# Hybrid mixer trunk: four stretches of fill in the state stage, both outputs in one bank, and new orders at the LRU, the branches and the second norm

## What is computed

```
h = RMSNorm(x) * (1 + scale1) + shift1
p = h @ W_in                        # columns split among four mixers
o_b = mixer_b(p slice)              # RG-LRU, stick-breaking attention, gated DeltaNet, RWKV-7
x = x + gate1 * ( sum_b sigmoid(h W_gate_b + b_gate_b) * (o_b W_branch_b) ) @ W_out
h = RMSNorm(x) * (1 + scale2) + shift2
x = x + gate2 * ( (gelu(conv(h W_gate)) * (h W_up)) @ W_down )
final RMSNorm
```

```
u = u_first - w S            # new values, w from the keys
o = q S + (q k) u            # output
S = decay * S + k u          # new state
```

## Time and profile before

| | |
|---|---|
| runs | 1933.66, 1928.02, 1931.73 us; median 1931.73 |
| the profiled execution | 1933.4 us, span 1931.5 us |
| mean granted clock of PE | 0.994 |
| busy: PE, DVE, ACT, POOL | 97%, 48%, 24%, 48% of the span |
| chain that ended last | PE 84%, DVE 8%, ACT 2%, POOL 2%, transfers 2% |

### The profile page before, as it was taken

One profiled execution on the slowest core, in us unless ns is written; L12 is line 12 of the kernel. 1 busy time (PEld: TensorE's weight loads), 2 busy tenths in 40 slices (PEclk: granted clock), 3 DMA queues, 4 the chain that ended last, 5 costly groups with the idle time before them and its releaser, 6 DMA issues.

```text
span 1931.5 us, 33600 instructions
## 1 busy us (share of the span) xinstructions
PE 1880.7 (97%) x14138; PEld 1499.8 (78%) x14138; DVE 935.9 (48%) x1443; ACT 467.2 (24%) x731; POOL 921.6 (48%) x1100
## 2 busy tenths in 40 slices
PE   6999999999999999999999899999999999999997
PEld 3778777767787887887887787788888888888885
DVE  3965578754546546545545825532332322323326
ACT  3432344451212213213214314310110101101103
POOL 2876556523223223323324574464655555655655
PEclk9999999999999999999999999999999999999999
DMA  8625211232222122122135521111111111111112
GB/s 337 213 77 185 98 55 66 82 125 79 66 68 78 52 83 78 40 94 78 41 105 196 206 100 33 33 44 55 43 54 43 54 44 54 44 52 45 45 53 87
DMA packets 69976, 163.51 MB, mean 85 GB/s; under 512 B 6112, under 2 KB 30816, under 8 KB 69856
## 3 DMA queue, kind: packets, MB, share of 16 engines
q1 hardware_dynamic: 62368, 142.88, 22.2%
q10 hardware_dynamic: 7488, 18.88, 2.6%
HBM read 133.17 MB, written 28.57 MB: 84 GB/s over the span
## 4 chain that ended last, share of the span: by engine, by line
PE 84%; DVE 8%; issue 2%; ACT 2%; POOL 2%; DMA 2%; SPq 0%; DVEq 0%; ACTq 0%; POOLq 0%
PE gbank L632 55%; PE mbank L1205 11%; PE mbank L957 3%; DVE state L2170 1%; PE gbank L1104 1%; POOL w_lo L530 1%; DVE fa L1920 1%; PE gbank L957 1%; PE mbank L713 1%; PE mbank L880 1%; PE gbank L734 1%; PE gbank L1160 1%; DVE fa L1843 1%; POOL w_hi L526 1%; DMA fa<-in_w_ada 1%
## 5 line engine op out<-in xcount | busy, mean ns | idle before, releaser
L526 POOL TENSOR_TENSOR w_hi<-w_raw,zero 128x256 fp32r<-128x256 f32 (+1 forms) x508 | 387.6, 794 | 937.5 <-PE gbank L632 770.5
L632 PE MATMUL gbank<-h_hi,w_hi 128*128 128x512 f32 x1648 | 659.1, 400 | 2.7 <-ACT fa L1300 2.7
L632 PE MATMUL gbank<-h_lo,w_hi 128*128 128x512 f32 x1648 | 649.7, 394 | 0.0
L632 PE MATMUL gbank<-h_hi,w_lo 128*128 128x512 f32 x1648 | 649.1, 394 | 0.0
L530 POOL TENSOR_TENSOR w_lo<-w_raw,w_hi 128x256 fp32r<-128x256 f32 (+1 forms) x508 | 459.7, 936 | 10.0
L632 PEld LDWEIGHTS gbank<-h_hi,w_hi 128*128 128x128 f32 x1648 | 310.3, 188 | 80.7 <-issue 17.6
L632 PEld LDWEIGHTS gbank<-h_hi,w_lo 128*128 128x128 f32 x1648 | 310.4, 188 | 67.2 <-issue 1.5
L632 PEld LDWEIGHTS gbank<-h_lo,w_hi 128*128 128x128 f32 x1648 | 310.5, 188 | 65.8 <-issue 2.9
L1205 PE MATMUL mbank<-ra,w_hi 128*128 128x512 f32 x640 | 197.1, 389 | 0.0
L1205 PEld LDWEIGHTS mbank<-ra,w_hi 128*128 128x128 f32 x640 | 120.1, 188 | 25.0
L2337 DVE SCALAR_TENSOR_TENSOR fa<-mbank,mod,fa 128x1024 f32<-128x1024 f32 x40 | 51.3, 1283 | 169.3 <-PE mbank L1205 169.3
(11 more groups left out here) (356 smaller groups left out, 2209.1 us busy)
## 6 DMA issues: line engine op xcount, KB each, us to landing
w_raw<-in_w_tail SPq DMA_DIRECT2D x74, 512.0 KB, 3.5
fa<-in_w_ada SPq DMA_DIRECT2D x48, 512.0 KB, 6.2
w_raw<-in_w_in SPq DMA_DIRECT2D x26, 512.0 KB, 3.7
p_scr<-fa ACTq DMA_DIRECT2D x20, 512.0 KB, 2.7
...
```

The lines of the kernel that those rows point to most:

```text
L526: last = pool.tensor_tensor(hi[:, c], raw[:, c], zero[:, 0:1].to_broadcast([P, w]), ALU.add)
L632: mm = pe.matmul(gb[bank], w, r, start=(q == 0), stop=(q == 3 * ks - 1))
```

## The change

1. Table `FILL`: the state stage has four stretches of fill in place of seven. They lie after `key_norm`, after `gd_sums`, between L1077 and L1080, and after L1080. The three that went were after `r3`, after from_state(0) and after `gd_norm`. The numbers of the stretches before the state stage are shifted too.
2. State stage on PE: all of `r3` first, then all of `u_first`, with an event of its own; w S before q S in `from_state`, with a wait of PE for its own `u_first`; both outputs in bank 3. ACT copies `uw` in two halves.
3. On DVE `prep_bonus` comes after next_state(0); in the last block both `o_lo`.
4. Start: shift and scale in four parts of 128 columns, loads of `w_ada1` after x tile 6 has landed, DVE's norms in pairs; parts 2 and 3 on PE after tiles 1 and 2 of the first two units.
5. LRU: ACT's copy of the result stands after the copies of the next unit (`lru_out_hi`); `ADA_EARLY` goes from 35 to 31, with four fewer tiles inside the LRU's first half and `ADA_BEHIND` changed.
6. Branches: DVE multiplies for t before it adds for t - 1. Out: tile 6, then 21 products of unit 1, tile 7, then the rest.
7. Second norm: DVE multiplies by root and scale in one operation, ACT adds the shift and rounds in one, DVE's rest takes the shift in.

```diff
-ADA_EARLY = 35
+ADA_EARLY = 31
 ADA_SLOT = [(8, 16, 18, 19)[_t % 4] if _t < ADA_EARLY else 12 + _t % 4 for _t in range(48)]
-ADA_BEHIND = {4: (20, 24), 5: (24, 28), 6: (28, 32), 7: (32, ADA_EARLY), 11: (ADA_EARLY, 39), 12: (39, 43), 13: (43, 48)}
+ADA_BEHIND = {4: (20, 24), 5: (24, 28), 6: (28, ADA_EARLY), 11: (ADA_EARLY, 35), 12: (35, 41), 13: (41, 48)}
...
-FILL = {False: ((10, 22, 36, 41, 48), (58, 68, 78, 88, 96), 104, (114, 120, 130, 140, 156, 174, 192)),
-    True: ((12, 26, 42, 50, 58), (72, 86, 100, 113, 123), 130, (138, 144, 153, 160, 173, 183, 192)),
-    "first": ((120, 134, 150, 158, 166), (180, 194, 208, 222, 236), 248, (258, 264, 274, 284, 300, 318, 336)),
-    "full": ((10, 22, 38, 43, 50), (64, 78, 92, 106, 116), 122, (130, 140, 152, 168, 184, 200, 216))}
+FILL = {False: ((10, 22, 36, 41, 48), (60, 72, 83, 94, 104), 114, (132, 152, 172, 192)),
+    True: ((12, 26, 42, 50, 58), (74, 89, 103, 117, 128), 138, (150, 164, 178, 192)),
+    "first": ((120, 134, 150, 158, 166), (184, 200, 215, 230, 245), 258, (276, 300, 318, 336)),
+    "full": ((10, 22, 38, 43, 50), (64, 78, 92, 106, 116), 126, (142, 164, 190, 216))}
...
-             + _INV_P * 4 + ["inv_Y", "inv_ZT", "r3"]
-             + ["ws"] + _SUM + ["+rw_p2", "ws", "+gd_g1"] + _SUM + ["+gd_g2", "rw_m1", "gd_m", "rw_m2"]),
...
+             + _INV_P * 4 + ["inv_Y", "inv_ZT", "r3", "u_first"]
+             + ["ws", "y_state"] + _SUM + ["+rw_p2", "ws", "y_state", "+gd_g1"] + _SUM + ["+gd_g2", "rw_m1", "gd_m", "rw_m2"]),
...
-           + ["new_u", "+rw_bonp"] + ["rw_S"] * 4 + ["gd_S"] * 4
-           + ["+rw_ar", "+rw_ar", "+rw_km", "new_u", "+rw_bm", "+rw_tl", "+rw_tl"] + ["rw_S"] * 4 + ["gd_S"] * 4
+           + ["new_u"] + ["rw_S"] * 4 + ["gd_S"] * 4
+           + ["+rw_bonp", "+rw_ar", "+rw_ar", "+rw_km", "new_u", "+rw_bm", "+rw_tl", "+rw_tl"] + ["rw_S"] * 4 + ["gd_S"] * 4
...
+        sp.wait_ge(sem("x_in6"), 16)
         for t in range(16):
-            if t >= 8:
-                sp.wait_ge(sem("ada_used"), t - 7)
-            sp.dma_start(fa[:, 12 + t % 8, :], a["w_ada1"][t]).then_inc(sem(f"ada1_in{t % 8}"), 16)
+            part, d = divmod(t, 4)
+            if part >= 2:
+                sp.wait_ge(sem("mod_used"), KT * (part - 2) + 2 * d + 2)
+            sp.dma_start(fa[:, 12 + 2 * d:14 + 2 * d, part % 2 * HALF:(part % 2 + 1) * HALF],
+                         a["w_ada1"][part, d]).then_inc(sem(f"ada1_in{t % 8}"), 16)
             if t == 3:
                 sp.dma_start(par[:], a["par"]).then_inc(sem("par_in"), 16)
...
+        def shift_and_scale(part):
+            for d in range(KT):
+                if part >= 2 and d == 0:
+                    pe.wait_ge(sem("mod1"), part - 1)
...
-                pe.wait_ge(sem(f"ada1_in{d}"), 16 * (part + 1))
+                pe.wait_ge(sem(f"ada1_in{part % 2 * 4 + d // 2}"), 16 * (part // 2 + 1))
                 for j in range(4):
-                    last = pe.matmul(mb[2 + part][32 * j:32 * j + 32, 0:256], c_pad[:, 32 * d:32 * d + 32],
-                                     fa[:, 12 + d, 256 * j:256 * j + 256], start=d == 0, stop=d == KT - 1)
-                last.then_inc(sem("ada_used"), 1)
+                    last = pe.matmul(mod_bank(part)[32 * j:32 * j + 32, 0:P], c_pad[:, 32 * d:32 * d + 32],
+                                     fa[:, 12 + d, part % 2 * HALF + P * j:part % 2 * HALF + P * (j + 1)], start=d == 0, stop=d == KT - 1)
+                last.then_inc(sem("mod_used"), 1)
...
-            for n in range(2):
-                last = pe.matmul(mb[2 + part][:, 256 + 4 * n:260 + 4 * n], fa[:, 10, part * 256 + n * P:part * 256 + (n + 1) * P],
-                                 m_("ident")[:, 0:P:32], start=True, stop=True)
-            last.then_inc(sem("mod_cols"), 1)
+            pe.matmul(mod_bank(part)[:, P:P + 4], fa[:, 10, part * P:(part + 1) * P], m_("ident")[:, 0:P:32], start=True,
+                      stop=True).then_inc(sem("mod_cols"), 1)
...
-        shift_and_scale(0, 0, KT)
+        shift_and_scale(0)
         turn_shift_and_scale(0)
-        shift_and_scale(1, 0, 4)
+        shift_and_scale(1)
         pe.wait_ge(sem("w_split"), 2)
         for k in range(KT):
             pe.wait_ge(sem("h_done"), k + 1)
             for s in range(2):
-                if k == 2 and s == 1:
-                    turn_shift_and_scale(1)
+                if k in (0, 2, 3) and s == 1:
+                    turn_shift_and_scale(max(1, k))
                 for hf in range(2):
...
-            if k < 2:
-                shift_and_scale(1, 4 + 2 * k, 6 + 2 * k)
+            if k in (1, 2):
+                shift_and_scale(k + 1)
...
-            for nm, off, b_, rhs, key in (("rw", 0, rw, rw["x"], rw["tokVA"][:, 256:512]), ("gd", 256, gd, gd["vb"], gd["kbe"])):
...
+            mixers = (("rw", 0, rw, rw["x"], rw["tokVA"][:, 256:512]), ("gd", 256, gd, gd["vb"], gd["kbe"]))
+            pe.wait_ge(sem("gd_TT"), at("gd_TT", i, 5))
+            for nm, off, b_, rhs, key in mixers:
...
             last.then_inc(done("r3", i), 1)
-            gates(i, FILL_STATE[0])
+            for nm, off, b_, rhs, key in mixers:
+                for h in range(4):
...
+            last.then_inc(done("u_first", i), 1)
...
+            y_bank = {"gd": mb[3][:, 0:256], "rw": mb[3][:, 256:512]}
...
-                    pe.wait_ge(sem("uw"), at("uw", i))
-                if par_:
-                    pe.wait_ge(sem("gd_Yd"), at("gd_Yd", i, 1))
-                for nm, st, yb in (("gd", 1, 3), ("rw", 0, 2)):
...
+                    pe.wait_ge(sem("u_first"), at("u_first", i))
+                    pe.wait_ge(sem("uw"), at("uw", i, 1))
...
                 last.then_inc(done("ws", i), 1)
+                if par_ == 0:
+                    pe.wait_ge(sem("uw"), at("uw", i))
+                else:
+                    pe.wait_ge(sem("gd_Yd"), at("gd_Yd", i, 1))
+                for nm, st in (("gd", 1), ("rw", 0)):
...
+                            last = pe.matmul(y_bank[nm][r:r + 64, y_], state[r:r + 64, st, t, r:r + 64], q_,
+                                             start=nm == "gd" and par_ == 0 and t == 0, stop=True, skip_group_check=True)
+                last.then_inc(done("y_state", i), 1)
...
+                pe.wait_ge(sem("y_state"), at("y_state", i, par_ + 1))
...
             from_state(0)
-            gates(i, FILL_STATE[1])
             to_state(0)
             if i < NB - 1:
                 key_norm(i + 1)
-            gates(i, FILL_STATE[2])
+            gates(i, FILL_STATE[0])
             from_state(1)
             if i < NB - 1:
                 gd_norm(i + 1)
-            gates(i, FILL_STATE[3])
             to_state(1)
             if i < NB - 1:
                 gd_sums(i + 1)
-            gates(i, FILL_STATE[4])
+            gates(i, FILL_STATE[1])
...
-        for k in range(6, KT):
-            first_out_tile(k)
+        first_out_tile(6)
+        pe.wait_ge(sem("w_split"), OUT_POS[1] + 1)
+        pe.wait_ge(sem("gated"), 6 * NB - 1)
+        gemm(1, 1, 0, h_hi, h_lo, KT, 0, 3 * (KT - 1))
+        first_out_tile(7)
+        gemm(1, 1, 0, h_hi, h_lo, KT, 3 * (KT - 1)).then_inc(sem("half_done"), 1)
+        pe.wait_ge(sem("gated"), 6 * NB)
+        gemm(3, 1, 1, h_hi, h_lo, KT).then_inc(sem("half_done"), 1)
...
             for hf in range(2):
-                if m == 1:
-                    pe.wait_ge(sem("gated"), 6 * NB)
-                else:
-                    pe.wait_ge(sem("x1"), m * 2 + hf - 3)
+                pe.wait_ge(sem("x1"), m * 2 + hf - 3)
                 gemm(2 * hf + slot, slot, hf, h_hi, h_lo, KT).then_inc(sem("half_done"), 1)
-        for m in range(1, 6):
+        for m in range(2, 6):
...
+        def lru_out_hi(c):
             act.wait_ge(sem("lru_o"), c + 1)
             act.activation(ra[:, c, :], fa[:, 12, :], ACT.Copy).then_inc(sem("lru_hi"), 1)
...
-                act.wait_ge(sem("ada_used"), ADA_EARLY)
+                act.wait_ge(sem("ada_used"), ADA_EARLY - 16)
             for hf in range(2):
                 in_copy(u, 2 * hf + u % 2, hf)
             if u in LRU_BEHIND:
                 act.wait_ge(sem(f"gb2_read"), u + 1)
                 lru_gates(LRU_BEHIND[u])
+            if u - 1 in LRU_BEHIND:
+                lru_out_hi(LRU_BEHIND[u - 1])
...
-            act.activation(uw.rearrange("p (c n) -> p c n", c=2), mbank[:, 0::3, 0:256], ACT.Copy).then_inc(done("uw", i), 1)
+            for c in range(2):
+                act.activation(uw[:, c * 256:c * 256 + 256], mb[3 * c][:, 0:256], ACT.Copy).then_inc(done("uw", i), 1)
...
-            act.activation(fa[:, 12 + k % 4, c], fa[:, 12 + k % 4, c], ACT.Identity, bias=mod[:, 24 + k:25 + k],
-                           scale=a1[:, 8 + k:9 + k]).then_inc(sem("h_f32"), 1)
-            act.wait_ge(sem("h_f32"), n + 1)
-            act.activation(h_hi[:, k, c], fa[:, 12 + k % 4, c], ACT.Copy).then_inc(sem("h_hi"), 1)
```

(47 more changed lines are left out.)

97 lines of the change are left out of this document (44 added, 53 removed).

## The result

The changed kernel takes 1938.55 us (median of 20 runs, 1932.94 to 1941.02); the kernel before, run beside it, 1932.84 (20 runs). The ratio is 1.0027, with a 95% interval of 1.0020 to 1.0035: 5.2 us slower, clear of noise, but still within the 0.3% that I had called no change. The forecast was 1939.6. The profiled execution took 1940.77 us, span 1939.0, 7.5 more than the span before.

What follows compares the result with a forecast made beforehand. It took the matmul engine, busy 97% of the span, as the bound. Terms -4.3 -0.7 -2.2 +0 +12.7 +2.4 = +7.9 gave 1941.3 on the profiled 1933.4 us, 1939.6 for the median; forecast 1935 to 1944, range 1921 to 1948.

Steps and rivals of the forecast that it cites:

- State stage without the clock: State stage, all blocks: PE waits for VectorE's second new_u beside POOL, +12.7 us, +7.5 of it in blocks 1, 3, 5.
- Its start hangs on rw_dec of ScalarE: Blocks 1, 3, 5: VectorE's state update waits for rw_dec at 4.77 us, so eight updates end at 7.26.
- the 0.5 that was to come back later: Blocks 1, 3, 5: L1074's 0.43 wait behind ScalarE goes and a third removed stretch saves its way in.
- removal and exposure cancel: State stage up to the first fill: removed stretches win what exposed copies cost, 5.02 us against 4.98 before.
- Block 7: Last block's state stage: no norm products cover new_u(1), both subtractions precede it; stand between 0 and 3.4, taken 1.4 us.
- Clock: After the three stands of 3.4 us: each may bring a half clock at 1.6, half of them counted, +2.4 us.
- LRU: Projection at L632: the 2.7 us wait for ScalarE and the half clock behind it, 1.6, both go, -4.3 us.
- Branches: Branch products: new order hides only the 0.1 between multiplication and addition, -0.7 us (0 to 2.6).
- Second norm: Second norm: one ScalarE operation and no copy behind it shortens PE's 3.3 us wait, -2.2 us (0 to -3.5).
- Output: Output at L1118: the 2.4 us wait stays, as tile 6 still waits for lo(6); 0 change.
- Start: Kernel start: first norm 2.6 us sooner, offset by parts 2 and 3 inside the projection loop; 0, range -2.5 to +2.
- The first rival: State stage: VectorE's chain from new_u(0) to new_u(1) stays 9.25 us; state +4.6, total -2.6, 1929; chance 0.23.

Runs made afterwards that it cites:

- pool_late: Changed kernel with POOL's split of the next mix unit held back in blocks 1, 3, 5 until the second new_u is made: 1928.92 us, 8.5 faster than the changed kernel.
- after: The changed kernel itself, with the whole change against the kernel before: 1938.55 us, ratio 1.0027.
- state_only: Kernel before with parts 1 to 3 of the change alone: 1941.72 us against 1931.33, ratio 1.0054.
- o_lo_late: Changed kernel with both branch subtractions of block 7 behind the second new_u: 1934.53 us, 3.5 faster than the changed kernel.
- bonus_back: Changed kernel with the next block's bonus ahead of the first state update again: 1935.63 us, 2.5 below the changed kernel.
- fill_more: Changed kernel with 20 fill products instead of 12 ahead of from_state(1) in blocks 1, 3, 5, eight fewer behind: 1933.05 us, 3.7 faster than the changed kernel.
- start_only: Kernel before with part 4 (new start) alone: ratio 1.0004 to the kernel before.
- fixed_no_hold: Whole change plus the three state-stage edits of state_first, without holding back the w_ada1 loads: equals state_first.
- lru_out_norm: Kernel before with parts 5, 6 and 7 alone: 7.1 us faster than the kernel before.
- state_first: Changed kernel, POOL's split held back, block 7's subtractions behind the second new_u, second state update before next block's tails: 1925.44 us, 12 faster than the changed kernel.
- no_start_fixed: Start of the kernel before, all other parts of the change plus the three state-stage edits of state_first: 8.1 us faster than the kernel before.

## Why the prediction was right, and where its steps were not

The direction and the time came out (1939.6 forecast, 1938.55 measured; +7.9 forecast in the sum, +7.5 in the profile, +5.2 by the ratio). The mechanism was the one named, VectorE late with the second new_u beside POOL: pool_late takes POOL away and the stand goes. But that the total came so near is luck: the state stage was put 6.5 us too high and the clock 5.3 too low, and the output's -1.6 and the start's +1.8 cancel as well.

- **State stage without the clock: 12.7 forecast, 6.2 measured** (three times 1.63, block 7's 1.61, 0.15, less 0.49 in blocks 0, 2, 4). The step that failed is "Its start hangs on rw_dec of ScalarE". The update uses the rw_dec of its own block, made a block earlier; the bonus was what had waited for ScalarE. So the updates ended at 6.5 and not at 7.26, the first of the six operations was over before POOL slowed it, and the others came every 0.86, not 0.95: 5.0 us for six, not 5.7. The stand was 1.93, not 3.4. In blocks 0, 2 and 4 the same 1.5 us are what I had called a stand of 1.4; there was none. And the 0.5 that was to come back later did not: the wait of 0.43 behind ScalarE's work is gone, but at the same place (L1089) block 1 now has one of 0.53 for the second state update. Steps that held: `to_state` at 3.19 (3.13 forecast), w S at 1.73 (1.65), with PE's wait for its own products at about the 0.27 taken (the last product of u_first starts about 0.33 before w S, less the 0.06 from one small product to the next), and "removal and exposure cancel".
- **Block 7: 1.4 taken between 0 and 3.4, 1.50 measured.** The cause is as stated, both subtractions ahead of new_u.
- **Clock: +2.4 forecast, +7.7 in the profile** (2.3, 2.3 and 3.2). Half of three stands at 1.6 was the working. The share was fair: of the twelve stands of 1.74 to 1.94 in the profiles of after, state_only, o_lo_late and bonus_back, seven were followed by the half clock, and of the five of about 1.5 in block 7 (after, state_only, pool_late, fill_more, bonus_back) three. What failed is the price: 1.6 was that of one stretch of 3.42 us in the rows of before, and nine of these ten falls lasted 6.83 us. Block 7's stand was not counted either. The Trainium skill, "TensorE: Matmul & The Clock Gate", "What's actually happening", says that idleness takes the engine down; the traces agree in that every fall has idle time just before or at its start, and show that the same 1.93 us brings it in one block and not in the next.
- **LRU: -4.3 forecast, -4.2 measured.** Both halves came as stated: no wait at the projection, no half clock at 113 us. Of the four tiles moved behind it nothing shows. That ScalarE alone held PE is less sure than I had it: before the change POOL's `w_lo` for that unit ended at 110.28, only 1.1 us ahead of the product at 111.42, and in state_only and start_only, which keep the old LRU, POOL's `w_lo` is what ends the stand (2.34 and 3.09). Which half of part 5, the later copy or the four fewer tiles on VectorE, took the stand away was not run apart.
- **Branches: -0.7, measured -1.2. Second norm: -2.2, measured -1.3**; its wait went from 3.3 to 2.3. That the rest is VectorE's own pace is likely, but no run takes it apart.
- **Output: 0 forecast, -1.6 in the profile.** The wait at the first output tile stayed, as forecast (2.4, 2.3), but the half clock behind it did not come. It did in pool_late, bonus_back and fixed_no_hold (at 1107.9, 1112.6 and 1100.7 us), so it is not the reordering that removed it; and state_only, with the old order and no half clock there, takes the same 84.1 us. The new order gains nothing, and in five of the ten profiles that have it (lru_out_norm, state_first, o_lo_late, fill_more, no_start_fixed) PE stands 0.64 to 1.37 us for POOL's `w_lo` behind these products, in none of the four with the old order.
- **Start: 0 forecast, +1.8 in the profile, +0.8 with an interval from -1.2 to +2.5 by the run alone.** Within its range. The first norm did come earlier (2.9 us from the first product, 2.6 forecast), but not by "64 instead of 128 records at 0.058": the earlier trace rows and the eight records behind it are 64, and now there are 64 of half the width, 0.030 each (1.95 for all). That is 1.9 us less; 0.6 more is the wait for a load of w_ada, which is gone there.
- **Contention.** The Trainium skill, SBUF — State Buffer, "Who interferes with whom", was right on who blocks whom: the state updates, which read one operand from PSUM, took 1.22 for four without POOL and 1.21 beside it (pool_late, 585.13 to 586.34), and the operations with two SBUF inputs 0.42 to 0.43 without and 0.93 to 1.08 with it.

The first rival (VectorE's chain from the first new_u to the second as long as before, 9.25) was in fact the better account of the stage: the chain took 9.06 (575.00 to 584.06), and 4.6 us for the stage is nearer to 6.2 than 12.7 is. Its total was too low mainly by the clock, which it had put at nothing. "Within 0.3%" had a chance of 0.24, and that is where 5.2 us fall.
